# Products of constants in TensorE's waits: three blocks of a model on one core

## What is computed

```python
mod = jax.nn.silu(c) @ w_ada[i] + b_ada[i]
n1 = _rmsnorm(h, norm1_g[i]) * (1.0 + sc1) + sh1
h = h + g1 * _mixer(n1, ...)
n2 = _rmsnorm(h, norm2_g[i]) * (1.0 + sc2) + sh2
moe = _hier_moe(n2.reshape(bsz * seq, d), w_grp, b_grp, w_er, b_er, w1, w3, w2)
h = h + g2 * moe.reshape(bsz, seq, d)
...
for l in range(DEPTH_2):          # 2 layers
    h = rms_norm(x, norm1_g[l]); z = h @ w_in[l]
    o_a, o_b, o_c = mla_mixer(...), gla_mixer(...), s5_mixer(...)
    x = x + merged @ w_out[l]
    h2 = rms_norm(x, norm2_g[l])
    x = x + jnp.square(jax.nn.relu(h2 @ w_ff1[l])) @ w_ff2[l]
```

## Time and profile before

| | us |
|---|---|
| median of 3 executions | 2790.27 (2789.05 to 2794.97) |
| profiled execution, its time | 2790.74 |
| profiled execution, span | 2788.9 |
| PE busy | 2260.9 (81% of the span) |
| VectorE busy | 1031.4 (37%) |
| ScalarE busy | 693.8 (25%) |
| mean granted clock of TensorE | 0.888 |

### The profile page before, as it was taken

How to read it: one execution, slowest core, us unless ns; L and a number is a source line. 1 busy time by engine, 2 the same in 40 slices (tenths; PEclk the granted TensorE clock), 3 DMA queues, 4 the chain that set the end, 5 groups by cost and what they waited for, 6 DMA issues and landing times.

```text
span 2788.9 us, 31882 instructions
## 1 busy us (share of the span) xinstructions
PE 2260.9 (81%) x13027; PEld 1643.2 (59%) x13027; DVE 1031.4 (37%) x2106; ACT 693.8 (25%) x1057; POOL 27.3 (1%) x47
## 2 busy tenths in 40 slices
PE   7999989776666776666775887799999887799999
PEld 4876669732232333232331655578899655578899
DVE  1667736410000110010111356642653356632653
ACT  2135544300000000000001235322542235322542
POOL 0000000000000000000000100000000100000000
PEclk8999999888888888788888887899999988899999
DMA  8434516589999999999997131132453431132452
GB/s 303 151 123 151 181 61 204 193 352 421 422 421 421 421 421 422 420 422 420 418 421 305 46 114 46 61 146 96 152 182 109 130 115 45 61 143 99 151 182 106
DMA packets 174501, 631.45 MB, mean 226 GB/s; under 512 B 10816, under 2 KB 28768, under 8 KB 125200
## 3 DMA queue, kind: packets, MB, share of 16 engines
q1 hardware_dynamic: 173008, 628.07, 57.7%
q0 software_dynamic: 1344, 1.28, 0.2%
HBM read 628.28 MB, written 1.05 MB: 226 GB/s over the span
## 4 chain that ended last, share of the span: by engine, by line
PE 58%; DMA 27%; DVE 8%; ACT 3%; SPq 2%; issue 2%; DVEq 0%; ACTq 0%
PE pb L176 25%; DMA ring<-in_w 25%; PE pb L1779 5%; PE pb L1780 5%; PE pb L1781 5%; PE pb L1053 3%; PE pb L1027 3%; PE pb L1745 2%; SPq L940 1%; PE pb L1722 1%; PE pb L487 1%; PE pb L171 1%; PE pb L488 1%; PE pb L489 1%; PE pb L201 1%
## 5 line engine op out<-in xcount | busy, mean ns | idle before, releaser
L176 PE MATMUL pb<-ar,ring 128*128 128x256 f32 (+1 forms) x2960 | 708.1, 401 | 34.7 <-DMA ring<-in_w_in 16.1
L176 PEld LDWEIGHTS pb<-ar,ring 128*128 128x128 f32 (+1 forms) x2960 | 586.4, 200 | 156.5 <-issue 45.2
L1027 PE MATMUL pb<-ring,ar 128*32 128x512 f32 x2048 | 283.3, 710 | 127.7 <-DMA ring<-in_w 127.1
L1779 PE MATMUL pb<-act,parts 128*128 128x256 f32 x1152 | 332.2, 288 | 13.3 <-DVE act L2349 13.3
L1780 PE MATMUL pb<-act,parts 128*128 128x256 f32 x1152 | 328.4, 285 | 0.0
L1781 PE MATMUL pb<-act,parts 128*128 128x256 f32 x1152 | 328.1, 285 | 0.0
L1053 PE MATMUL pb<-ring,ar 128*32 128x512 f32 x1024 | 172.3, 834 | 120.0 <-DMA ring<-in_w 120.0
L1027 PEld LDWEIGHTS pb<-ring,ar 128*32 128x32 f32 x2048 | 77.0, 127 | 313.2 <-issue 312.5
L1779 PEld LDWEIGHTS pb<-act,parts 128*128 128x128 f32 x1152 | 222.4, 193 | 14.7 <-issue 14.1
L1780 PEld LDWEIGHTS pb<-act,parts 128*128 128x128 f32 x1152 | 222.3, 193 | 0.6
L1781 PEld LDWEIGHTS pb<-act,parts 128*128 128x128 f32 x1152 | 222.2, 193 | 0.0
(11 more groups left out here) (339 smaller groups left out, 2483.3 us busy)
## 6 DMA issues: line engine op xcount, KB each, us to landing
ring<-in_w SPq DMA_DIRECT2D x384, 1024.0 KB, 18.6
ring<-in_w_in SPq DMA_DIRECT2D x36, 2048.0 KB, 7.9
ring<-in_w_ff SPq DMA_DIRECT2D x32, 2048.0 KB, 8.9
ring<-in_w_ada SPq DMA_DIRECT2D x12, 2048.0 KB, 13.0
ring<-in_w_ssm_out SPq DMA_DIRECT2D x4, 2048.0 KB, 8.8
ring<-in_w_out SPq DMA_DIRECT2D x4, 2048.0 KB, 7.7
ring<-in_w_cv_out SPq DMA_DIRECT2D x2, 2048.0 KB, 8.1
ring<-in_w_mix_out SPq DMA_DIRECT2D x2, 2048.0 KB, 7.7
```

The lines of the kernel that those rows point to most:

```text
L176: ins = e.matmul(out, l, r, start=(i == 0), stop=(i == len(pairs) - 1))
L1027: ins = e.matmul(k.pb[b][32 * j:32 * j + 32, :], v.xg[i][:, kt, 32 * j:32 * j + 32], w[j][:, m, :], start=(kt == 0), stop=(kt == 7))
L1779: e.matmul(k.pb[b][:, 0:T], wh[:, kt, c0:c0 + 128], xh, start=(first and kt == 0), stop=False)
```

## The change

A function `idle` issues n fp32 products of two constants, 128x128 ones as the stationary block and the first 256 columns of another constant, into a PSUM bank; nothing reads them. `Ring.spare` gives the bank for it: the one that `take` would give next, with the wait for its reader, without taking it. `idle` is called at 13 places in the code; counted over blocks, layers and units, that makes 35 groups on PE. The other engines' instructions stay as they are.

```diff
+    def spare(self):
+
+        b = next(b for b in self.banks if b not in self.open)
+        if b in self.emptied:
+            self.e.wait_ge(*self.emptied.pop(b))
+        return b
...
+def idle(k, e, n, b):
+
+    for _ in range(n):
+        e.matmul(k.pb[b][:, 0:T], k.con("ones"), k.con("iota"), start=True, stop=True)
...
     for blk in range(4):
         if blk < 3:
+            idle(k, e, 8, ring.spare())
             ada_rows(k, e, ring, blk + 1)
...
+    idle(k, e, 14, ring.spare())
     e.wait_ge(*k.at("n1", 8))
...
     b = ring.take(("col", 0))
+    idle(k, e, 24, ring.spare())
     e.wait_ge(*k.at("rest", 1))
...
     lg = [ring.take(("lg", tt)) for tt in range(2)]
+    e.wait_ge(*emptied[3])
+    idle(k, e, 16, 3)
     for i in range(8):
         e.wait_ge(*k.at("n2", i + 1))
...
         b = ring.take(("place", tt))
+        if tt == 0:
+            idle(k, e, 10, 3)
         e.wait_ge(*k.at("asg", tt + 1))
...
             for b in range(3, 7):
                 e.wait_ge(*emptied.pop(b))
+        if q == QUADS - 1:
+            idle(k, e, 14, ring.spare())
         e.wait_ge(*k.at("swt", q + 1))
...
         if q == 0:
+            idle(k, e, 8, 3)
             e.wait_ge(*k.at("nt", 4))
...
         for half in range(2):
+            if q == QUADS - 1:
+                idle(k, e, 16, ring.spare())
             w = [slot(24 * q + 16 + 4 * half + j, [128, 2, 1024]) for j in range(4)]
...
+
+    emptied.clear()
+    emptied.update(kept)
     combine(QUADS - 1)
-
-    emptied.update(kept)
...
             b = ring.take(("unit", l, i))
             if i == 0:
+                idle(k, e, 36, ring.spare())
                 e.wait_ge(*k.at("n_in", 8 * l + 8))
...
                 yield 1, 1
+                idle(k, e, (24, 8, 16, 26)[2 * tt + i], ring.spare())
                 e.wait_ge(*k.at("roped", 4 * l + 2 * tt + i + 1))
...
     def inputs(u):
         c = u // 2
+        if u >= 3:
+            idle(k, e, 9, ring.spare())
         for q in range(2):
...
+            if u == 7:
+                idle(k, e, 26, ring.spare())
             e.wait_ge(*k.at("scanned", 8 * l + u + 1))
...
     for j in range(10):
+        if j == 2:
+            idle(k, e, 26, wide.spare())
         e.wait_ge(*k.at("ff_low", 2 * (NSPLIT * l + j + 1)))
```

## The result

The changed kernel took 2826.96 us (median of 4 runs, 2824.65 to 2830.74) against 2790.62 for the kernel before (4 runs beside it): the ratio is 1.0129, 95% interval 1.0111 to 1.0147, so it is slower by 36 us, 1.3%. The forecast was 2836, range 2811 to 2858. The profiled execution took 2824.65 with a span of 2822.3; before it was 2790.7 and 2788.9.

A forecast was written before the change was run, and what follows sets the result against it. TensorE was taken to set the pace except in the expert loop, which waits for weights; mixer +1.1, routing +1.8, expert loop's end +9.4, layer 0 +9.4 and layer 1 +23.5 sum to +45.2 on 2790.7: 2836, range 2811 to 2858.

The forecast's parts named there:

- The price: Every fill: one fp32 product takes two records, 0.433 us at full clock and 0.87 at 1.2 GHz.
- Rival B: Every fill: a product of constants costs one record, 0.217, so nearly all fills fit and the time is 2765; chance 0.05.
- The clock: Behind covered waits: half of the work at 0.50 comes back, −19.0 in layer 0 and −16.6 in layer 1.
- Rival C: Every fill: products of constants don't hold the clock, so all 43.7 of savings fail, 2864 to 2885; chance 0.07.
- Rival D: Whole kernel: the fills are hidden, their overrun absorbed by other waits, 2790; chance 0.04.
- The front of layer 1: Before layer 1's first unit: the fill of 36 starts after the weights land, 18.3 less 2.7 saved, +15.6.
- The end of the expert loop: Last w2 halves and combine: fills outlast the landings and the fill of 14 can't use the 3.8 wait, +9.4.
- two readings: Wait of 3.82 before `combine`: either the jump takes it, as the row suggests, or the jump is free, 4 less.
- the cycles: S5 cycles: each of four per layer gains 0.65 and loses 2.0 behind a new wait for `prob`, +5.4 a layer.
- Rival A: S5 cycles: new waits for `prob` don't lower the clock, or VectorE's slack takes the loss up, −16, 2820; chance 0.18.
- the routing: Routing before the expert loop: fills of 16 and 8 overrun their waits and the gather doesn't gain, +1.8.
- the front of the mixer: Condition's rows and n1: three fills of 8 at +1.0, the fill of 14 at +1.7, −3.0 back in clock, −0.3.

The follow-up runs named there:

- e11: The changed kernel, same counts and places, with idle's constants read as bf16 so that a product is one record: 2787.37 us, ratio 0.9990.
- e3: The changed kernel with fill counts cut to each wait's length, none before the combine, layer 1's front fill moved ahead of its weights' wait: 2756.08 us, ratio 0.9867.
- e1: The changed kernel without the fill of 36 at the front of layer 1: 2811.51 us, ratio 1.0075.
- e2: The changed kernel without the last quad's three fills (14 before the combine, 16 before each half of w2): 2814.72 us, ratio 1.0083.
- e7: The kernel before with 32 products put into the jumped-over section for overflow blocks, nothing more executed: 2787.08 us, ratio 0.9985.
- e5: e3 with added fills of 5, 8, 2 and 2 in front of each layer's four waits for `prob`: 2747.36 us, ratio 0.9858.
- e10: e3 without the ten fills of 8 in the S5 cycles: 2749.88 us, ratio 0.9857.
- e9: e5 plus fills in other open waits (mixer's filler, tail's weights, middle norm's first square, inner products): 2736.47 us, ratio 0.9808.
- e8: e3 with about half of each fill count: 2767.65 us, ratio 0.9923.
- e4: The kernel before with only the ten fills of 9 in the S5 cycles; the waits of `spare` elsewhere remain: 2795.21 us, ratio 1.0015.

## Why the prediction was right

**The price** was right: 36 products take 15.6 us by its sum, and 15.70 in the trace of layer 0's front; two records each. Rival B's price does not exist for this form, and with a form of one record, cheaper still (e11, 0.119), the time is 2787, not 2765, since the rival let short fills cover whole waits.

**The clock** was right: the mean rose from 0.888 to 0.927, full clock stands behind the long fills, and e3 turned that into 34 us. Rival C fell with it. **Rival D** fell with e1 and e2: what a fill overruns is hardly taken up later.

**The front of layer 1**, the largest term, was predicted at +15.6 and is +15.5 by e1 against the changed kernel. Between the two traces of before and after the shift grows by 14.2 (17.0 to 31.2 at 2175 of before): by 16.9 through the fill, less 2.8 that the units behind it give back, where the sum had 18.3 less 2.7. By 2204 only 12.5 of growth are left, since a later cold stretch (the clock is 0.72 from 2200 to 2206 of before) has gone. It has gone in e1 too (1.00 from 2215 to 2220 there), though e1 has no fill at this front; why, no run shows.

**The end of the expert loop** was predicted at +9.4 and is +10.0. The step that the fill of 14 can't use the 3.8 held in this kernel (0.70 and 3.50 of standing still). Its reason didn't: I took 3.8 as the time of the jump, and e2, e3 and e7 show 0.9 at the same jump. In the prediction's choice between two readings the row was the better guide for this kernel, and neither reading was the mechanism. Within the term, the sums' start was to move by 9.1 and moved by 11.7, as the fill's last part ran partly at half clock:

```profile
1518.90:1522.30 3.40, 3.40 (x9) 2.70 (x8) 0.00 (x0) 0.00 (x0) 0.00 (x0) 0.51 1.05 389
```

The sums then took 3.62 at full clock instead of 5.30, where I had counted 0.3 of loss.

**What was mis-sized: the cycles.** The prediction had +5.4 a layer, 4 x (−0.65+2.0), +10.8 in all. In the changed kernel the shift moves over them by −0.4 and −0.1, and by +0.2 in both layers together in e1 and in e2, which have the same fills there: the term is about nothing. The mechanism is there (the waits for `prob`, 0.50 behind some of them, 2.0 lost in the state's products), and e5 shows it by undoing it. Two things make it small. The waits are not 4.0 each: TensorE's list of waits sums up the eight of both layers.

```profile
PE pb L178 <- issue: 18.4, 8, 3.9
```

That is 2.3 on the mean, from 1.02 to 3.93. And not each of them has a cold stretch behind it. The very cycle that the prediction worked out looks like this in the changed kernel:

```profile
1753.75 5.41 PE L183 MATMUL pb<-ar,ring 128*128 128x256 f32 x16
1760.34 1.06 PE L178 MATMUL pb<-const,ring 128*128 128x128 f32 x8 [1.19 <-issue]
1761.34 2.81 PE L1779 MATMUL pb<-ar 128*32 128x256 f32 x16
```

The clock was at 0.50 in the unit ahead of the wait (from 1754.4 to 1757.8), which took 5.41 instead of 3.72; TensorE so came later to the wait for `prob`, which shrank to 1.19, and behind it the clock was full. It is the same in four of the eight cycles: the cold stretch lies ahead of the wait, which takes it up. One has none. Behind the other three the turn and the state's products take 2.5, 1.4 and 1.5 longer than before, 5.4 in all, where the prediction had eight times 2.0; the 5.2 that it had as the gain in front about balances that. The waits filled in e5 give back 6.0. I had taken every such wait to be followed by a cold stretch, and the loss to be wholly on the path.

**Rival A** had no loss from these waits, −5.2 for both layers. With −0.6 measured, the cycles came out nearer to it than to the forecast's +10.8, by the slack that it names. The cycles are 11.4 of the 13.3 by which the two layers came out below their terms. Another 3.1 lie at the front of layer 1 (+12.5 for +15.6), and the rest, +1.2, I can't assign to single waits.

**Mis-sized: the routing**, +1.8 predicted, −1.6 measured. The gather gave nothing, as predicted: from before 553.4 to 562.1 the shift goes from +4.9 to +4.7. Half of the difference is in the first experts' products behind it, whose shift falls from +4.7 to +3.0; I had held them as a possible loss. The other half lies ahead of the gather, where the shift grows by 0.3 only. There the sum had left out a term, the fill of 10 in front of "place", 4.3 us in a wait of 2.71 (the shift rises from +3.1 to +4.6 at it), and had counted too little for the clock: the routing's product takes 3.69 instead of 7.07, and the turn behind it is shorter too, 1.91 instead of 2.63.

**Mis-sized: the front of the mixer**, −0.3 predicted, +3.5 in the profiled execution, but 0.0 and −0.1 in those of e1 and e2, which have the same code there. The fill of 14 in the trace of the changed kernel, and then in that of e1:

```profile
38.51 9.14 PE L227 MATMUL pb<-const 128*128 128x256 f32 x28
```

```profile
37.92 6.29 PE L227 MATMUL pb<-const 128*128 128x256 f32 x28
```

In the first one the clock was at 0.50 while the fill ran (6.8 us of it, from 37.5 to 44.3). This term of a single profile differs by 3 to 4 us from one execution to the next.

In sum: −11.8 against the terms (−6.2 and −7.1 in the layers, −3.4 in the routing, +3.8 in the front of the mixer, +1.1 elsewhere), so +33.4 instead of +45.2. Nearly all of it, 11.4, is the cycles' term. The other terms together were to give +34.4 and gave +34.0; that they agree so well is luck in part, since the routing and the front of the mixer were off by as much in opposite directions, and a stage of one profile scatters by 3 to 4 us anyway (e10).

## What to carry to other kernels

Products that only keep TensorE busy do hold its clock, and here they are worth nearly 2% (e9, with the 3 to 4.5 us of the code's place in it) if each fill is as long as its wait and stands in front of it: count them from the wait's length in the trace and the price of one from a row of the same form. An overrun costs its full length where the engine paces the program (36 products behind a landed weight: 15.5 us; 15 in front of the wrong square: 5.7), and a fill that ended 3.3 us early left 3.4 us of cold stretch out of 3.9 (e8). After filling one wait, look in the new trace for where it has moved, and fill that (e5), before judging the first.

## What the runs showed that was not expected

Behind the jump over the overflow blocks TensorE stood for 3.82 in the kernel before with no releaser, 3.50 in the changed one, 4.11 in e1, 1.50 in e4 and 5.39 in e11, and not at all in e2, e3 and e5 to e10, though e7 executes nothing that the kernel before doesn't. The trace's queues for instructions show two transfers of 16 KB around it: in the kernel before they start at 1504.1 and 1507.7, and the sums at 1510.3, 2.6 behind the second; in e7 at 1505.5 and 1509.1, and the sums at 1508.9, before the second. In the changed kernel, in e1, e4 and e11 one or two records of a product ran, then came the standstill, and the next record started 2.3 to 2.5 behind the start of the second transfer. In e2 too the sums start less than 1 behind the second, too early to need it. This fits a first piece that ends at or just behind the jump's target in some kernels and holds all of the sums in others. That the code's place decides whether TensorE stands is shown by e7; that the end of the fetched piece does it, and that these transfers are TensorE's, is read from the starts and was not tried at other places. For such a kernel a difference of 3 us between versions can be this alone.
